# Router scores of a hybrid decoder step: product in both column halves of PE, halves added in the turn, sigmoid read from PSUM, half of the norm's scaling on Pool

## What is computed

```python
h2 = rmsnorm(x, lw['g_norm_ffn']) * (1.0 + scale_f) + shift_f
x = x + gate_f * moe_ffn(h2, lw)
...
scores = jax.nn.sigmoid(jnp.einsum('td,de->te', h, w_router).astype(jnp.float32))
choice = scores + b_router.astype(jnp.float32)
grp = choice.reshape(-1, N_EXPERT_GROUPS, N_EXPERTS // N_EXPERT_GROUPS)
grp_score = jnp.sum(lax.top_k(grp, 2)[0], axis=-1)
...
_, idx = lax.top_k(jnp.where(emask > 0, choice, -jnp.inf), TOP_K)
w = jnp.take_along_axis(scores, idx, axis=-1)
w = w / jnp.sum(w, axis=-1, keepdims=True) * ROUTED_SCALE
```

## Time and profile before

| what | value |
|---|---|
| median of 3 runs | 977.28 us (977.1 to 978.26) |
| the profiled execution, its own time | 978.77 us |
| its span | 976.9 us |
| PE busy | 949.4 us (97%) |
| PE weight loads | 531.7 us (54%) |
| DVE busy | 563.2 us (58%) |
| ACT busy | 201.6 us (21%) |
| POOL busy | 102.6 us (11%) |
| q1, the queue of SyncE and ScalarE, of 16 engines' span | 76.8% |
| TensorE clock granted | 0.999 of full |

### The profile page before, as it was taken

The page is one execution under the profiler, slowest core; times in us unless marked ns, Lnnn a source line. Parts: engine busy times, 40 slices in busy tenths (PEclk is TensorE's granted clock), DMA queues, the critical chain, the costliest instruction groups (busy, mean ns, idle before and its releaser), DMA issues.

```text
span 976.9 us, 14989 instructions
## 1 busy us (share of the span) xinstructions
PE 949.4 (97%) x5200; PEld 531.7 (54%) x5201; DVE 563.2 (58%) x1404; ACT 201.6 (21%) x414; POOL 102.6 (11%) x76
## 2 busy tenths in 40 slices
PE   7999999999999999999999999999999999999997
PEld 3488867544446788888653443444344344344343
DVE  2613322478854011123737787878878778878764
ACT  3311231335435100002511111111111111111111
POOL 0100010100000000000112122112212212211100
PEclk9999999999999999999999999999999999999999
DMA  8995569756655493544689999999999999999993
GB/s 310 419 416 221 181 207 312 224 154 171 170 155 242 156 375 149 215 154 191 241 331 418 428 424 425 424 422 424 426 426 425 423 424 422 429 422 427 425 426 141
DMA packets 54608, 311.97 MB, mean 319 GB/s; under 512 B 9018, under 2 KB 28506, under 8 KB 33426
## 3 DMA queue, kind: packets, MB, share of 16 engines
q1 hardware_dynamic: 48338, 297.28, 76.8%
q0 software_dynamic: 5904, 12.79, 3.7%
q10 hardware_dynamic: 304, 1.08, 0.3%
HBM read 315.80 MB, written 3.95 MB: 327 GB/s over the span
## 4 chain that ended last, share of the span: by engine, by line
PE 71%; DMA 18%; SPq 6%; DVE 3%; issue 2%; ACT 0%; DVEq 0%
PE bank L844 42%; PE pA L844 18%; DMA ring<-in_w_e_gu 14%; PE pB L844 5%; PE pC L844 4%; SPq L487 3%; DMA ring<-in_w_ada 2%; PE pD L844 1%; SPq L531 1%; DMA ring<-in_w_bg 1%; SPq L526 1%; DMA pT<-in_poolT 1%; PE pA L1413 0%; DVE xT L2469 0%; DVE hT L2342 0%
## 5 line engine op out<-in xcount | busy, mean ns | idle before, releaser
L844 PE MATMUL pA<-ring,qT 128*64 128x512 f32 x976 | 228.7, 596 | 6.2 <-DMA ring<-in_w_e_gu 5.9
L2452 DVE STREAM_TRANSPOSE qT<-xs 32x256 f32<-32x256 f32 x480 | 209.2, 436 | 7.7
L844 PE MATMUL bank<-hT,ring 128*128 128x264 f32 (+1 forms) x832 | 189.8, 388 | 0.9 <-DMA ring<-in_w_bg 0.8
L844 PEld LDWEIGHTS bank<-hT,ring 128*128 128x128 f32 (+1 forms) x832 | 154.2, 189 | 31.8 <-issue 4.7
L844 PEld LDWEIGHTS pA<-ring,qT 128*64 128x64 f32 x976 | 69.9, 137 | 137.7 <-issue 119.8
L816 POOL DMA_INDIRECT xs<-h_rows,idx x32 | 80.6, 2517 | 370.4 <-DVE idx L2432 274.6
L844 PE MATMUL bank<-wuk,ring 128*128 128x512 f32 x192 | 86.3, 597 | 0.0
L844 PE MATMUL bank<-pT 128*128 128x256 bf16 (+1 forms) x499 | 85.4, 273 | 0.2 <-issue 0.2
L844 PE MATMUL bank<-pT,vtok 128*128 128x256 bf16 (+1 forms) x264 | 71.8, 281 | 0.0
L844 PE MATMUL pB<-ring,oaT 128*64 128x512 f32 x240 | 62.0, 605 | 0.0
L844 PE MATMUL pC<-ring,oaT 128*64 128x512 f32 x240 | 60.3, 592 | 0.0
(11 more groups left out here) (359 smaller groups left out, 913.5 us busy)
## 6 DMA issues: line engine op xcount, KB each, us to landing
ring<-in_w_e_gu SPq DMA_DIRECT2D x59, 2048.0 KB, 20.7
ring<-in_w_e_dn SPq DMA_DIRECT2D x34, 1024.0 KB, 17.0
ring<-in_w_e_dn SPq DMA_DIRECT2D x13, 2048.0 KB, 19.3
ring<-in_poolT SPq DMA_DIRECT2D x64, 208.0 KB, 2.7
ring<-in_w_ada SPq DMA_DIRECT2D x12, 1024.0 KB, 10.7
ring<-in_w_bg SPq DMA_DIRECT2D x4, 3072.0 KB, 11.2
ring<-in_w_mix SPq DMA_DIRECT2D x5, 2048.0 KB, 9.8
ring<-in_w_ada SPq DMA_DIRECT2D x4, 2048.0 KB, 12.9
```

The source lines that it names most:

```text
L844: return nc.tensor.matmul(out, lhsT, rhs, start=start, stop=stop)
L2452: last = V.transpose(xTs[32 * j:32 * j + 32, q % 2, :, 32 * a:32 * a + 32], src[32 * a:32 * a + 32, j])
```

## The change

- The router's eight products write in turn to the rows 0 to 63 (even tiles) and 64 to 127 (odd tiles) of their bank, each half summing four tiles. The norm's product comes after all eight. `lgT` therefore has 128 partitions, and both halves get half of each score.
- VectorE multiplies both halves by `rstd`, and adds the shifts of the prompt (formerly ScalarE's bias) and of the samples. `twice` is the sum of the identity's two column halves, 128x64. The turn of the scores is a product with it, not a transpose: it adds the halves. It waits for `raw`.
- ScalarE takes the sigmoid of the turned scores from the PSUM bank straight into `lg`, after the second of its eight `hT` rows; VectorE's three copies go, and it waits for `lsig` at 2.
- The multiplies `hT = xa * rstd` for tiles 4 to 7 are on Pool, ahead of its two memsets; Pool waits for the root and no longer for `var`.

```diff
@@ build
-        lgT = abuf[0:E, 0:NT]
+        lgT = abuf[:, 0:NT]
+        twice = abuf[:, NT:NT + E]
@@ gpsimd (the semaphore "zeroed" is called "pooled" now, everywhere)
-            pool.wait_ge(s["var"], 5)
-            nc.gpsimd.memset(xs[:], 0.0).then_inc(s["zeroed"], 1)
-            pool.wait_ge(s["zeroed"], 2)
+            pool.wait_ge(s["root"], 5)
+            for k in range(DT // 2, DT):
+                nc.gpsimd.tensor_tensor(hT[:, k, 0:NP_], xa[:, k, 0:NP_], rstd[:, 0:NP_], ALU.mult).then_inc(s["pooled"], 1)
+            nc.gpsimd.memset(xs[:], 0.0).then_inc(s["pooled"], 1)
+            pool.wait_ge(s["pooled"], 6)
             pool.wait_ge(d_vout, 16 * 2)
-            nc.gpsimd.memset(gmf, 0.0).then_inc(s["zeroed"], 1)
+            nc.gpsimd.memset(gmf, 0.0).then_inc(s["pooled"], 1)
@@ tensor
+            def router():
+
+                n = BASE["rout"]
+                t = enter(n)
+                for k in range(DT):
+                    pe.wait_ge(s["xa"], k + 1)
+                    o = E * (k % 2)
+                    last = mm(t[o:o + E, 0:NB], wrou[:, k, :], xa[:, k, :], k < 2, k >= DT - 2)
+                last.then_inc(full[n % 4], 1)
+                pe.wait_ge(s["tilesum"], 6)
+                mm(pB[:, 0:NT], ones[:], sq[:, 0, :], True, False)
+                pe.wait_ge(s["sq2"], DT)
+                mm(pB[:, 0:NT], ones[:], sq[:, DT - 1, :], False, True).then_inc(s["norm2"], 1)
+
             def scaled(stage, np_, w):
...
                 for k in range(DT):
                     pe.wait_ge(s["xa"], k + 1)
                     last = mm(t[0:np_, 0:NB], w(k), xa[:, k, :], k == 0, k == DT - 1)
-                    if stage == "rout" and k == 3:
-                        pe.wait_ge(s["tilesum"], 6)
-                        mm(pB[:, 0:NT], ones[:], sq[:, 0, :], True, False)
-                        pe.wait_ge(s["sq2"], DT)
-                        mm(pB[:, 0:NT], ones[:], sq[:, DT - 1, :], False, True).then_inc(s["norm2"], 1)
...
-            scaled("rout", E, lambda k: wrou[:, k, :])
+            router()
...
-            pe.wait_ge(s["lsig"], 1)
+            pe.wait_ge(s["raw"], 1)
             for j, m in enumerate((P, P, NS)):
-                last = nc.tensor.transpose(t[0:m, j * E:(j + 1) * E], lgT[:, j * P:j * P + m], ident[0:E, 0:E])
+                last = mm(t[0:m, j * E:(j + 1) * E], lgT[:, j * P:j * P + m], twice, True, True)
@@ scalar
-            act.wait_ge(s["raw"], 1)
-            nc.scalar.activation(lgT[:, NP_:NT], lgT[:, NP_:NT], ACT.Sigmoid)
-            nc.scalar.activation(lgT[:, 0:NP_], lgT[:, 0:NP_], ACT.Sigmoid, bias=shifts[0:E, 0, 0:1]).then_inc(s["lsig"], 1)
             for k in range(DT):
-                act.wait_ge(s["h2x"], k + 1)
+                if k == 2:
+                    n = BASE["routT"]
+                    t = fulls(n)
+                    nc.scalar.activation(lg[0:NS, 2, :], t[0:NS, 2 * E:3 * E], ACT.Sigmoid).then_inc(s["lsig"], 1)
+                    nc.scalar.activation(lg[:, 0:2, :], t[:, 0:2 * E].rearrange("p (j e) -> p j e", j=2), ACT.Sigmoid
+                                         ).then_inc(s["lsig"], 1)
+                    act.wait_ge(s["lsig"], 2)
+                    act.sem_inc(free[n % 4], 1)
+                if k < DT // 2:
+                    act.wait_ge(s["h2x"], k + 1)
+                else:
+                    act.wait_ge(s["pooled"], k - DT // 2 + 2)
                 nc.scalar.activation(hT[:, k, 0:NP_], hT[:, k, 0:NP_], ACT.Identity, bias=ada[:, 3, k, 0:1]
@@ vector
             V.memset(posm, 0.0)
+            V.tensor_tensor(twice, ident[:, 0:E], ident[:, E:P], ALU.add)
...
-            raw("rout", E, lgT, 0)
-            for k in range(DT):
+            n = BASE["rout"]
+            t = fulls(n)
+            V.tensor_copy(shifts[:, 0], t[:, NT:NB])
+            link(V.tensor_tensor(lgT, t[:, 0:NT], rstd[:], ALU.mult))
+            dve.sem_inc(free[n % 4], 1)
+            V.tensor_scalar(lgT[:, 0:NP_], lgT[:, 0:NP_], shifts[:, 0, 0:1], None, ALU.add)
+            link(V.tensor_tensor(lgT[:, NP_:NT], lgT[:, NP_:NT], shifts[:, 0, 1:NC], ALU.add))
+            dve.sem_inc(s["raw"], 1)
+            for k in range(DT // 2):
                 V.tensor_tensor(hT[:, k, 0:NP_], xa[:, k, 0:NP_], rstd[:, 0:NP_], ALU.mult).then_inc(s["h2x"], 1)
...
-            n = BASE["routT"]
-            t = fulls(n)
-            for j, m in enumerate((P, P, NS)):
-                last = V.tensor_copy(lg[0:m, j, :], t[0:m, j * E:(j + 1) * E])
-            link(last)
-            dve.sem_inc(free[n % 4], 1)
+            dve.wait_ge(s["lsig"], 2)
             link(V.tensor_tensor(ch[:], lg[:], rows(brou[:], 3), ALU.add))
```

More of the change, by code:

```diff
@@ L430, in build @@
         s = {n: sem(n) for n in (
-            "consts", "zeroed", "csig", "csilu", "ada_mm", "ada", "sq1", "var", "root", "h1s", "h1", "eksq", "ekss", "tilesum", "adsum", "mix_done", "in_done", "gsig",
+            "consts", "pooled", "csig", "csilu", "ada_mm", "ada", "sq1", "var", "root", "h1s", "h1", "eksq", "ekss", "tilesum", "adsum", "mix_done", "in_done", "gsig",
             "sqq", "latn", "krin", "krot",
@@ L754, in _ @@
             nc.gpsimd.memset(ones[:], 1.0).then_inc(s["consts"], 1)
-            nc.gpsimd.memset(onecol[:], 0.0).then_inc(s["zeroed"], 1)
-            pool.wait_ge(s["zeroed"], 1)
+            nc.gpsimd.memset(onecol[:], 0.0).then_inc(s["pooled"], 1)
+            pool.wait_ge(s["pooled"], 1)
             nc.gpsimd.memset(onecol[:, 1:2], 1.0).then_inc(s["consts"], 1)
@@ L1361, in clear_sums @@
                     pe.wait_ge(free[n % 4], n // 4 + 1)
-                pe.wait_ge(s["zeroed"], 3)
+                pe.wait_ge(s["pooled"], 7)
                 pe.wait_ge(s["h2tok"], 6)
@@ L2506, in _ @@
             at[0] = chain[0]
-            dve.wait_ge(s["zeroed"], 3)
+            dve.wait_ge(s["pooled"], 7)
             index(0, None)
```

## The result

| what | before | after |
|---|---|---|
| median, measured side by side | 977.7 us (977.1 to 978.26, 8 runs) | 980.22 us (978.63 to 982.37, 8 runs) |
| ratio after to before, 95% interval | | 1.0024 (1.0013 to 1.0036) |
| the profiled execution, its own time | 978.77 us | 979.05 us |
| its span | 976.9 us | 977.2 us |
| PE busy | 949.4 us | 947.6 us |

The change makes the kernel slower by 0.24%, 2.3 us on 977.7 (1.3 to 3.5), and its median lies 0.3 above the predicted range. The two spans differ by only 0.3 us, and that has to be taken apart first: the router's first product starts at 463.83 in this execution and at 464.92 in the one of before, though the program up to it is hardly touched. These 1.1 us are variation between executions: in r1, the changed kernel again, the same product starts at 465.07. So from here on all distances are counted from the router's first product.

A forecast was written before the change was run, and what follows sets the result against it. The end was taken to follow the routing chain, which sets when the expert-weight stream becomes full, microsecond for microsecond. Terms 0.8 + 0.3 − 0.55 gave +0.6; 977.28 + 0.6 = 977.9 us, range 976.3 to 979.9.

The forecast's parts named there:

- d: Shift of `chcm<-lg,brou`, the first step of the expert choice; forecast 0.8 + 0.3 − 0.55 = +0.6 us.
- Step 1: Router on PE: all eight products, paired side by side, precede the norm's product, making the norm 0.8 us later.
- Rival D: Router's halves on PE don't overlap, so the norm is 1.2 us later still: +1.8, 979.1 us; chance 0.05.
- Step 2: Logits on VectorE: the prompt columns' shift becomes one more instruction there, 0.3 us more.
- Step 3: From first `hT` multiply to choice, now waiting for ScalarE's table load and sigmoids: 3.15 instead of 3.70, 0.55 us less.
- rival A: Pool's and VectorE's two-input instructions block each other from the logits on: +0.45 to +1.0 us, middle 978.6; chance 0.35.
- Step 4: Four `hT` multiplies on Pool, 0.53 us each (0.42 to 1.1), covered by ScalarE's work; later memsets delay nobody.
- Rival C: Code load on Pool before the third gather: free below 20 us, 990 us if 33; chance of over 2 us 0.05.
- Step 5: `h2` on ScalarE: ready at 478.7 instead of 476.0, second group of transposes 0.3 us later, nothing added to the sum.

The follow-up runs named there:

- r5: The kernel before with the norm's reciprocal made three times instead of once on VectorE; 980.8 us, ratio 1.0036.
- r11: r9 plus one tiny Pool addition ahead of the memsets, so the code load falls into idle time; 976.3 us against 978.49 before, ratio 0.9979.
- r9: r8 with Pool's memsets moved ahead of the root, right behind the norm's product; 983.99 us, ratio 1.006.
- r8: Changed kernel with norm's product after sixth router product, early sigmoid table, sigmoids after first `hT` row, Pool multiplies after VectorE's sample rows; 977.71 us, ratio 0.9999.
- r6: The changed kernel with the norm's product after the router's sixth product instead of the eighth; 979.23 us, ratio 1.0018.
- r7: r2 with Pool's memsets also waiting until VectorE's logits are done; 978.87 us, ratio 1.0012.
- r2: The changed kernel without its Pool part, all eight `hT` multiplies on VectorE; 979.88 us, ratio 1.0019.
- r10: The changed kernel with a one-column sigmoid right behind the root, loading ScalarE's sigmoid table there; 978.97 us, ratio 1.0015.
- r12: r11 with all eight multiplies on VectorE, Pool doing only memsets and no small addition; 978.18 us, ratio 1.0006.

## Why the prediction was wrong

The structure held and two terms of the sum did not.

**What bounds the kernel: right.** The end follows the routing chain 1 to 1: +3.5 for +3.67 in r5, −2.1 (−3.0 to −1.0) for −1.28 in r11, +5.9 (4.6 to 7.1) for +6.74 in r9, and 445.0 to 446.9 us from the gates' turn to the transfer of the late chain in all fourteen profiles. That spread of 1.8 us is as large as the change's own shift, so the weight lies on r5, r9 and r11. One correction: what counts is the gates' turn, not `chcm`, to which I tied d "since from there on the program is unchanged". In r8 the program between was unchanged too, and 1.6 us were lost in it to a memset.

**Step 1, the norm's product: right.** 0.8 predicted, 0.93 measured, 0.97 gained back in r6. The halves overlap: 14 records in 2.06 us are seven products, where eight records, four products, took 2.06 before. Rival D falls.

**Step 2, the logits: half right.** The TENSOR_SCALAR was priced 0.3 and takes 0.35. The addition behind it was to keep its 0.16 and takes 0.68.

**Step 3, from the logits to the choice: the step that failed.** 3.15 predicted, 3.74 measured; the predicted gain of 0.55 was a loss of 0.04. The path is as described (two multiplies, two rows of ScalarE, table, sigmoids, and VectorE idle for over a microsecond before `chcm`), but ScalarE's second row starts 1.52 behind the first multiply and not 0.83. What carried the errors of steps 2 and 3 is an assumption that the forecast never states, that VectorE's rows keep their lengths beside Pool's. Its opposite was rival A, to which I gave 0.35 and whose price I put at +0.45 to +1.0; measured it is 0.52 on the addition and 0.69 on ScalarE's second row, +1.2. My price was reckoned with Pool multiplies of 0.53 us, and they last 0.635 to 0.834; how much of the excess is their length and how much the moments at which the rows meet, no run separates. A's addition in full, laid over the forecast, gives 977.9 + 1.2 = 979.1, and the changed kernel's median in r1 was 979.58, when first measured 980.22. Of the 2.3 us by which the latter lies above 977.9, 1.17 is d (1.77 instead of 0.6), 0.42 the kernel before (977.7 instead of 977.28), and 0.7 is left to scatter. So the number missed narrowly, and r1's lies inside my range, but that is no credit to the forecast: the range's upper part was A's.

**Why A was undervalued.** My evidence against it was VectorE's multiplies at an even 0.34 beside a memset, and I wrote myself that a memset reads nothing. It was evidence for another case, and r7 shows it so: two-input rows pass a memset untouched and not a multiply. SBUF — State Buffer of the Trainium skill (section "Who interferes with whom") states it in just these cases: a VectorE instruction with two SBUF inputs contends with a Pool instruction that reads SBUF and not with one that only writes, and a `tensor_scalar` in its two-port mode contends with any; whoever starts first keeps the ports. The traces agree three times, the last on the assumption that the row runs in that mode, which no view names: 0.68 for 0.16 and 2.70 for 1.43 beside multiplies, 0.97 for 0.35 beside a memset. Between a rule that named the case and rows that did not show it, the chance belonged with the rule.

**Step 4, Pool.** The multiplies take 0.635 to 0.834 us, within my 0.42 to 1.1 and above the 0.53 taken; 2.62 for four beside the first rows of the choice in r8. The memsets end at 476.2 and harm nobody in the changed kernel. Rival C fits here (third gather 501.05, 37.22 behind the router's first product and 35.42 before, later by just the chain) but its size was open to 33 us and is 6 to 9: 6.25 us idle ahead of the reduction, 7.17 in r11, 9.23 in r9. The GPSIMD Engine Reference of the Trainium skill (section 2.1) puts the first call of freshly loaded code at some 6 us; the idle times ahead of the reduction agree, 6.15 to 6.70, and those of r11 and r9 are longer. I had not used that figure.

**Step 5, `h2`: right.** Ready at 478.84 (478.7 predicted), the second group of transposes at 478.90.

**Open.** The time differences of the table lie above the chain's shift in five kernels of the change's family (r2, r6, r7, r10, r12) by 0.6 to 1.0 us, each shift inside or within 0.1 us of its interval, and below it in r9 and r11 by 0.8 to 0.9. Whether that is chance or a small cost of the changed rows elsewhere, these runs don't settle. Why r9's load takes 9.23 us isn't settled either: it was issued at 470.0, ahead of the wait for VectorE's rows, and yet the multiplies start 5.9 behind the end of those rows at 473.3, as if it had begun there.

## What to carry to other kernels

Work halved between VectorE and Pool in the same microseconds gained nothing here, where both read two tensors from SBUF (2.70 us for four beside four, 2.77 for eight alone): plan Pool's share into a stretch where VectorE waits or reads PSUM, and look at what Pool does next too, since its memset held up a TENSOR_SCALAR from SBUF to SBUF (0.97 for 0.35 in r2) as its multiply held up a two-input row. When a first two-input instruction goes to Pool, which cost 5.8 us of waiting in r9, find the idle time where its code load can lie, and put a tiny instruction there. And when evidence against a rival comes from a neighbouring operation, ask whether the neighbour uses the same resource.

## What the runs showed of the hardware

- **Block by kind of row.** Pool multiply against VectorE with two SBUF inputs: 128x8 addition 0.68 for 0.16, four 128x256 multiplies 2.16 to 2.70 for 1.43. Pool memset against VectorE TENSOR_SCALAR from SBUF to SBUF: 128x256 0.97 for 0.35, the pair of 128x36 1.98 for 0.40. Pool multiply against TENSOR_SCALAR: 128x64, three, 1.88 for 0.58 (r9). Pool memset against two-input multiplies: nothing (2.77 both ways). Pool memset against RECIPROCAL from SBUF to SBUF: nothing (1.80 both ways in r9, r11 and r12), and Pool multiplies against the MAX8 rows of the choice: nothing (1.73 both ways in r8 and r11), so a row is not held up for having one input. Reads of PSUM, such as the scaling of the router's product beside Pool's first multiply (0.42), stay as they were.
- **One row that kept its length.** In the changed kernel the TENSOR_SCALAR at 471.41 has its 0.35 though Pool's first multiply runs from 470.81 to 471.54. In r2 the row that was held ended 0.15 behind the memset's end; by that this one could have ended at 471.69, and it ends at 471.76 anyway, so a wait would not be seen.
- **TensorE's clock after an idle stretch.** In r9 TensorE did nothing from 476.8 to 482.5; the granted clock fell to 0.50 and stayed there until 487, and a group of transposes took 1.06 for 0.60.
- **The load of code on Pool** has no busy row. Its issue is to be seen as two rows `MODIFY_POOL_CONFIG` on Pool's queue (in the changed kernel at 304.7, by the view of L804, and at 492.6 and 492.7, by that of L827), its duration as idle time marked `<-issue` or charged to a releaser long past: 6.15 to 6.70 us ahead of the reduction in nine profiles, 7.17 ahead of the first addition in r11.
